# Head of a transformer step: caches loaded later, tokens turned earlier; last expert group: throw-away matmuls and one output moved up

## The reference

```python
mod = silu(c) @ w_mod + b_mod                     # c: latent or context; w_mod 1024 x 6144
shift1, scale1, gate1, shift2, scale2, gate2 = split(mod, 6)
h = rms_norm(x, g_attn) * (1.0 + scale1) + shift1
qa, ka, va, qb, kb, vb, ga, gb = split(h @ w_in)  # w_in 1024 x 4352
# attention over cached keys and values (256 tokens) and the step's own; differential
# attention with lam = exp(sum(lq1*lk1)) - exp(sum(lq2*lk2)) + 0.2
```

```python
for e in range(16):                               # expert-choice: 64 latent + 16 context rows each
    ye = silu(xe @ w_gate[e]) * (xe @ w_up[e]) @ w_down[e] * gates[e]
y[rows[e]] += gate2 * ye                          # scattered into x
out = rms_norm(y, g_final)
```

## Time and profile before

| what | value |
|---|---|
| median of three runs | 1245.5 us (1245.05 to 1246.2) |
| the profiled execution | 1246.18 us, span 1244.4 us |
| mean granted clock of TensorE | 0.981 |
| PE busy | 1188.5 us, 96% of the span |
| PE's weight loads | 854.5 us, 69% |
| DVE busy | 915.1 us, 74% |
| ACT busy | 721.6 us, 58% |
| POOL busy | 176.7 us, 14% |
| HBM read, written | 269.64 MB, 15.73 MB |

### The profile page before, as it was taken

One profiled execution on the slowest core, in us unless ns is written; L12 is line 12 of the kernel. 1 busy time (PEld: TensorE's weight loads), 2 busy tenths in 40 slices (PEclk: granted clock), 3 DMA queues, 4 the chain that ended last, 5 costly groups with the idle time before them and its releaser, 6 DMA issues.

```text
span 1244.4 us, 17367 instructions
## 1 busy us (share of the span) xinstructions
PE 1188.5 (96%) x6056; PEld 854.5 (69%) x6056; DVE 915.1 (74%) x1145; ACT 721.6 (58%) x1029; POOL 176.7 (14%) x154
## 2 busy tenths in 40 slices
PE   4899999999999999999899999999999999999994
PEld 2578877778777777778486667666676666766662
DVE  2674559899683323444778999899997999979995
ACT  3433347777641221223667876777766777667774
POOL 3143340000000000010400111100113111111110
PEclk9999999999999999999889999999999999999997
DMA  9852241110424443471648998999989999799995
GB/s 359 262 198 68 68 98 43 33 33 22 172 79 149 143 117 124 179 289 68 220 164 319 380 383 317 307 371 383 383 276 320 369 385 385 262 331 366 375 385 190
DMA packets 110862, 291.62 MB, mean 234 GB/s; under 512 B 29265, under 2 KB 30498, under 8 KB 110274
## 3 DMA queue, kind: packets, MB, share of 16 engines
q1 hardware_dynamic: 106576, 273.16, 60.5%
q0 software_dynamic: 3792, 12.86, 4.1%
q10 hardware_dynamic: 418, 4.63, 0.9%
HBM read 269.64 MB, written 15.73 MB: 229 GB/s over the span
## 4 chain that ended last, share of the span: by engine, by line
PE 88%; DVE 5%; ACT 3%; DMA 3%; issue 1%; SPq 0%; POOL 0%; ACTq 0%; DVEq 0%; POOLq 0%
PE ps L1228 14%; PE ps L1229 14%; PE ps L1230 14%; PE ps L742 9%; PE ps L744 9%; PE ps L743 9%; PE ps L956 2%; DMA raw<-in_w_mod_dram 2%; PE ps L940 2%; DVE neg_max L1861 2%; PE ps L1181 1%; PE ps L979 1%; PE ps L1182 1%; PE ps L975 1%; DVE q_lo_t L1853 1%
## 5 line engine op out<-in xcount | busy, mean ns | idle before, releaser
L1952 DVE TENSOR_TENSOR raw_lo<-raw,w_hi 128x1024 fp32r<-128x1024 f32 x256 | 304.9, 1219 | 44.6 <-ACT w_hi L1587 33.0
L1587 ACT ACTIVATE w_hi<-raw 128x1024 fp32r<-128x1024 f32 x252 | 264.8, 1059 | 80.1 <-PE ps L1230 78.4
L1228 PE MATMUL ps<-w_hi,xe_hi 128*80 128x512 f32 x512 | 204.6, 400 | 0.0
L1230 PE MATMUL ps<-w_hi,xe_lo 128*80 128x512 f32 x512 | 203.2, 397 | 0.0
L2408 POOL DMA_INDIRECT x_dram<-y_g,rows_e x15 | 87.9, 5858 | 504.4 <-DVE y_g L2181 504.4
L1952 DVE TENSOR_TENSOR extra_lo<-extra,w_hi 128x1024 fp32r<-128x1024 f32 x128 | 152.5, 1219 | 8.2 <-ACT w_hi L1587 7.3
L1587 ACT ACTIVATE w_hi<-extra 128x1024 fp32r<-128x1024 f32 x128 | 135.9, 1064 | 37.8 <-PE ps L1230 37.5
L742 PE MATMUL ps<-w_hi,ht 128*128 128x512 f32 (+1 forms) x330 | 129.5, 392 | 1.8 <-DVE ht L1754 1.8
L744 PE MATMUL ps<-w_hi,ht 128*128 128x512 f32 (+1 forms) x330 | 126.3, 383 | 0.0
L743 PE MATMUL ps<-raw_lo,ht 128*128 128x512 f32 (+1 forms) x330 | 126.2, 382 | 0.0
L522 DVE TENSOR_TENSOR raw_lo<-raw,w_hi 128x1024 fp32r<-128x1024 f32 x48 | 57.7, 1225 | 79.5 <-ACT w_hi L517 78.9
(11 more groups left out here) (322 smaller groups left out, 2026.9 us busy)
## 6 DMA issues: line engine op xcount, KB each, us to landing
raw<-in_w_exp_down_dram SPq DMA_DIRECT2D x112, 512.0 KB, 6.3
raw<-in_w_exp_gate_dram SPq DMA_DIRECT2D x80, 512.0 KB, 5.4
extra<-in_w_exp_up_dram SPq DMA_DIRECT2D x64, 512.0 KB, 5.7
raw<-in_w_exp_up_dram SPq DMA_DIRECT2D x64, 512.0 KB, 5.5
extra<-in_w_exp_gate_dram SPq DMA_DIRECT2D x48, 512.0 KB, 5.2
raw<-in_w_in_dram SPq DMA_DIRECT2D x16, 1024.0 KB, 5.5
raw<-in_w_mod_dram SPq DMA_DIRECT2D x12, 1024.0 KB, 6.8
raw<-in_w_mod_dram SPq DMA_DIRECT2D x16, 512.0 KB, 11.3
```

The lines of the kernel that those rows point to most:

```text
L1228: pe.matmul(b, stat_hi, hi[:, cols], start=(k == 0), stop=False)
L1230: mm = pe.matmul(b, stat_lo, hi[:, cols], start=False, stop=(k == KD - 1))
L1587: act.activation(w_hi[:, (DENSE_SPLITS + h) % NHL, :], expert_half(h), ACT.Copy)\
L1952: dve.tensor_tensor(expert_lo_half(h), expert_half(h), w_hi[:, (DENSE_SPLITS + h) % NHL, :].bitcast(F32), ALU.subtract).then_inc(s_lo, 1)
```

## The change

It has seven edits. (1) POOL loads the first key cache only when part chunk (1, 1) has landed, and makes the parts of the first cached keys and loads the second cache behind all its other loads. (2) ACT squares all five token tiles before it brings turned tiles out of PSUM. (3) PE's order in the head: two tokens are turned ahead of chunk (0, 1), two ahead of (0, 2), one ahead of (0, 3), `spin` matmuls whose result nobody reads stand between, the six matmuls on `w_hi` go to bank 1, part chunk (1, 0) moves ahead of `first_step(0)`. (4) The second row is turned within `first_step(2)`, between its token tiles 1 and 2. (5) The first half of the second gemm chunk is done one k tile at a time, `first_step(4)` and `first_step(5)`, so `product(0, ...)` begins with half 3. (6) DVE makes the next two low halves before the lambda sums instead of behind them. (7) In the last group PE runs 5 `spare` matmuls before the turns of expert 15's hidden rows and 6 behind them, and DVE scales expert 14's output before two splits instead of behind them.

```diff
@@ -713,7 +713,7 @@
                 nh = halves_of(j)
                 _, n, kt = GEMMS[j]
                 per = HALF // n
-                for hh in range(0 if j else 2, nh):
+                for hh in range(0 if j else 3, nh):
                     h = gemm_half(j, hh)
                     if before_half and (j, hh) != (5, 0):
                         before_half(hh)
@@ -833,21 +833,29 @@
             pe.transpose(bank(5, 0, 81), vec[:, :], ident[0:81, 0:81]).then_inc(s_vect, 1)
             pe.wait_ge(s_ct, 1)
             pe.wait_ge(s_dve, 2)
+            def spin(n):
+
+                for _ in range(n):
+                    pe.matmul(bank(1, 0, P), ident, ident, start=True, stop=True)
+
             part_chunk(0, 0)
-            part_chunk(0, 1)
-            pe.wait_ge(s_tab2, 16)
+            spin(8)
             turn_tokens(0)
             turn_tokens(1)
-            part_chunk(0, 2)
+            spin(8)
+            part_chunk(0, 1)
             turn_tokens(2)
             turn_tokens(3)
+            part_chunk(0, 2)
+            turn_tokens(4)
             part_chunk(0, 3)
-            turn_tokens(4)
+            pe.wait_ge(s_tab2, 16)
+            spin(6)
             part_turn(0)
             pe.wait_ge(s_hi, 1)
-            pe.wait_ge(s_xtd, NT)
             for _ in range(6):
-                pe.matmul(bank(5), w_hi[:, 0, 0:P], w_hi[:, 0, 0:NW], start=True, stop=True)
+                pe.matmul(bank(1), w_hi[:, 0, 0:P], w_hi[:, 0, 0:NW], start=True, stop=True)
+            part_chunk(1, 0)
 
             def hth(k, tt):
                 return ht[:, HT_HI[k], tt]
@@ -873,28 +881,32 @@
                     turn_keys(("b", 1, 0))
                     turn_keys(("b", 1, 1))
 
-            def first_step(k):
+            def first_step(k, between=None):
 
                 h = gemm_half(0, k // 2)
                 pe.wait_ge(s_lo, SPLIT_OF[h] + 1)
                 pe.wait_ge(s_htl, k + 1)
                 hi, lo = hi_half(h, NW)[:, k % 2, :], lo_half(h, NW)[:, k % 2, :]
                 for t in range(NT):
+                    if t == 2 and between:
+                        between()
                     b, tt = bank(t), slice(t * P, (t + 1) * P)
                     pe.matmul(b, hth(k, tt), hi, start=(k == 0), stop=False)
                     pe.matmul(b, hth(k, tt), lo, start=False, stop=False)
                     mm = pe.matmul(b, htl(k, tt), hi, start=False, stop=False)
                 return mm
 
+            pe.wait_ge(s_xta, NT)
+            pe.wait_ge(s_xtd, NT)
             first_step(0)
-            part_chunk(1, 0)
             part_chunk(1, 1)
             first_step(1)
             part_chunk(1, 2)
             part_chunk(1, 3)
-            first_step(2)
-            part_turn(1)
+            first_step(2, between=lambda: part_turn(1))
             first_step(3).then_inc(s_half, 4 // 2)
+            first_step(4)
+            first_step(5).then_inc(s_half, 1)
             product(0, hth, htl, before_half=lambda hh: pe.wait_ge(s_htl, 2 * hh + 2))
             turn_keys(("a", 0, 0))
             turn_keys(("b", 0, 0))
@@ -1219,6 +1231,12 @@
                                           ident[0:EROWS, 0:EROWS])
                     mm.then_inc(s_htr, 1)
 
+                def spare(n):
+
+                    for _ in range(n):
+                        pe.matmul(bank(0, 0, EG * EROWS, slice(0, EROWS)), xe_hi[:, 0, 0:EROWS], xe_hi[:, 0, :],
+                                  start=True, stop=True)
+
                 def half_product(h, banks, stat_hi, stat_lo, k, sides=(0, 1)):
                     pe.wait_ge(s_lo, i * GH + DENSE_SPLITS + h + 1)
                     hi, lo = w_hi[:, (DENSE_SPLITS + h) % NHL, :], expert_lo_half(h)
@@ -1249,8 +1267,13 @@
                                 pe.wait_ge(s_silu2, i * 8 + 2 * EG)
                                 gather_context(i + 1)
                                 gather(i + 1, 0)
+                            if last:
+                                pe.wait_ge(s_silu2, i * 8 + 2 * EG)
+                                spare(5)
                             turn_hidden(e, 0)
                             turn_hidden(e, 1)
+                            if last:
+                                spare(6)
                             if not last:
                                 gather(i + 1, 1)
                                 gather(i + 1, 2)
@@ -1301,10 +1324,8 @@
                 if t:
                     act.wait_ge(s_ss, t)
                 act.activation(squares[:, :], x_n[:, t, :], ACT.Square, accum_out=ss[:, t:t + 1]).then_inc(s_ss, 1)
-                if t >= 2:
-                    evict_tokens(t - 2)
-            evict_tokens(NT - 2)
-            evict_tokens(NT - 1)
+            for t in range(NT):
+                evict_tokens(t)
             split_hi(act, SPLITS[0])
             act.wait_ge(s_xta, NT)
             act.wait_ge(s_xtd, NT)
@@ -1780,6 +1801,7 @@
                                          ALU.mult)
 
 
+            lead(0, HALVES_B, 2)
             dve.wait_ge(s_bc, 16 * 6)
             dve.tensor_scalar(g_qk[:, 0, :], g_qk[:, 0, :], SCALE, None, ALU.mult).then_inc(s_dve, 1)
             own()
@@ -1788,8 +1810,6 @@
             dve.wait_ge(s_dve, own())
             dve.tensor_reduce(lam[:, 0:2 * HB].rearrange("p (a h) -> p a h", a=2), pairs[:, :, 0], AX.X, ALU.add)\
                .then_inc(s_lamw, 1)
-
-            lead(0, HALVES_B, 2)
             dve.wait_ge(s_lame, 1)
             dve.tensor_tensor(lam[:, 2 * HB:], lam[:, 0:HB], lam[:, HB:2 * HB], ALU.subtract).then_inc(s_dve, 1)
             dve.wait_ge(s_dve, own())
@@ -2192,9 +2212,12 @@
                         if before == "u" and k == 0:
                             hidden(e1, 0)
                             hidden(e1, 1)
+                        early = last and (before, e1) == ("d", EG - 2)
+                        if early and k == 0:
+                            output(e1)
                         if not last or h + LEAD < GH:
                             expert_lo(h + LEAD, i)
-                        if before == "d" and k == 1 and (n or not first):
+                        if before == "d" and k == 1 and (n or not first) and not early:
                             output(e1)
                         if before == "u" and kind == "g" and k in (4, 5):
                             hidden_lo(e1, k - 4)
@@ -2271,7 +2294,6 @@
                 pool.dma_start(k_cache[:, KVA:, :].rearrange("p m d -> p (m d)"),
                                cache_diff_k[0, 0, rows].rearrange("p h i d -> p (h i d)")).then_inc(s_kc[n], 16)
 
-            load_key_cache(0)
             def one_over_rms(dst, sums, count_of, semaphore):
 
                 pool.tensor_scalar(dst, sums, 1.0 / count_of, EPS, ALU.mult, ALU.add).then_inc(s_pool, 1)
@@ -2305,10 +2327,9 @@
                     make_parts(("b", n, g), k_cache[:, KVA + 4 * g:KVA + 4 * g + 4, :])
 
 
-            pool.wait_ge(s_kc[0], 32)
-            make_cached_parts(0)
-            pool.wait_ge(s_kparts, 3)
-            load_key_cache(1)
+            second_half = CHUNK["part", 1, 1]
+            pool.wait_ge(s_raw[second_half % NRAW], raw_count[second_half])
+            load_key_cache(0)
             for n, src in enumerate((lambda_q1, lambda_k1, lambda_q2, lambda_k2)):
                 flat = src.rearrange("a h d -> a (h d)")
                 pool.dma_start(lam_w[:, n, :, :].rearrange("p h d -> p (h d)"), flat.to_broadcast([P, HB * HD]))\
@@ -2319,6 +2340,10 @@
                 .then_inc(s_vac, 16)
             pool.dma_start(vb_n[:, 0:2, :], cache_diff_v[0, 0].rearrange("(t p) h d -> p t (h d)", p=P))\
                 .then_inc(s_vc, 16)
+            pool.wait_ge(s_kc[0], 32)
+            make_cached_parts(0)
+            pool.wait_ge(s_kparts, 3)
+            load_key_cache(1)
 
             for t in range(NT):
                 pool.wait_ge(s_qss, t + 1)

```

## The result

The changed kernel took 1238.49 us (median of five, 1237.35 to 1240.56), the kernel before 1245.25 us beside it (1243.32 to 1246.2): ratio 0.9946, 95% interval 0.9932 to 0.996. Forecast: 1239.0.

A forecast was written before the change was run, and what follows sets the result against it. The prediction took the head to be bound by DMA, with PE carrying 88% of the chain. Head -5.0 and last group -1.6 sum to -6.6: 1245.5 - 6.6 = 1238.9, say 1239 us; range 1233.5 to 1242.5.

The forecast's parts named there:

- bound by DMA at (1, 3): Head, second row's last chunk: lands at 37.4 instead of 45.05 us, read from 37.8; 6.3 us won.
- part_turn(0) at 24.5: Head, first row's turn on PE: runs at 24.5 us instead of 29.71, with spins filling idle time.
- The hole: Slow DMA stretch while g_qk loads finish: moves to 39.0 to 43.0 us, so chunk (gemm 0, 1) lands at 46.5.
- Idle 4.1 us, clock cost 1.8: Ahead of first_step(4): PE stands from 46.7 to 50.8 us, then slow matmuls cost 1.8 (0 to 2.5).
- The cap: ACT's squares behind the lambda sums: square 4 at 65.9 us, product 1 no earlier than 67.3, 6.0 below 73.25.
- Head -5.0, tail -1.6: Product 0 ends at 66.6 instead of 71.65 us; last group's spare matmuls hold the clock, saving 1.6.
- A: Head: slow stretch does not follow g_qk loads, (gemm 0,1) lands at 42.7, head -9.7, time 1234 us; chance 0.22.
- B: Head: (1,3) stays behind the hole, landing at 45; time 1240.7 us; chance 0.12.
- C: Head, slower: the hole grows, meeting three waiting chunks; 1248 us with a hole of 13 us; chance 0.04.
- D: Nothing measurable: lower clock also behind find_rows at 802, last group's drop may stay; 1243.9 us; chance 0.07.

The follow-up runs named there:

- the list alone: Kernel before with only GpSimd's (POOL's) new load order, first key cache after part chunk (1, 1): 1243.28 us, ratio 0.9985.
- three traces: Traces of three versions of the changed kernel: no spare matmuls (1238.32 us), lambda sums first (1237.59), expert 14's output late (1237.53).
- The version with all rows different: Changed kernel with all six lambda and g_qk loads reading 128 different rows instead of one row 128 times; computes other values; ran once, 1237.98 us.
- the version with the loads moved away: Changed kernel with all six one-row loads (four lambda, two g_qk) moved behind the second key cache: 1232.97 us, ratio 0.9913.
- the version with GpSimd's old list: Changed kernel with GpSimd's (POOL's) load order put back as in the kernel before, the other edits kept: 1243.09 us, ratio 0.9987.
- one version: Changed kernel with only the two g_qk loads reading 128 different rows instead of one row 128 times; computes other values; ran once, 1234.94 us.

## Why the prediction was right, point by point

**The kernel is bound by DMA at (1, 3), and the list frees it.** Right as to the landing: forecast 37.4, measured 37.2. But it reads as if the 6.3 us were won by the list, and the list alone won 1.9. PE waited only 0.71 us for this chunk before, and what makes its early landing pay is PE's new order.

**part_turn(0) at 24.5.** Wrong by 1.8: it ran at 26.26, though chunk (0, 0) began 0.7 us earlier than before (9.63 for 10.32) where the working has it "as before". I counted a spin as one instruction of 0.12 us; it is two, and the second group took 1.95 us for what I put at 1.0. By the trace without spins, they push part_turn(0) by 2.2 us and pay 0.6 back at part_turn(1).

**The hole moves onto (gemm 0, 1), which lands at 46.5.** The mechanism was right, and the landing at 46.2 to 46.4 in three traces. In the profiled one it was 45.0. I tied the hole to the g_qk loads alone, but the lambda loads make half of it. The Trainium skill (DMA: Bandwidth & Descriptors, Why small descriptors are slow) puts the bus overhead of a 256-byte descriptor at 27%, so small rows cost little by it. The version with all rows different agrees, at 320 GB/s and more; that rule is about size and does not speak of one row read again and again, which is what made the hole here.

**Idle 4.1 us, clock cost 1.8.** The end of the wait was forecast at 50.8 and came at 50.5 to 50.7 in the three traces. PE got there later, so it waited 2.2 to 2.3, not 4.1, and the low clock still came and cost 1.54. In the profiled execution of the changed kernel the wait was 0.42 and there was no low clock. This is the step that missed in that trace: 1.5 us of the end of the wait (49.28 for 50.8) and 1.8 of the clock, 3.2 in all at the first key turn (63.40 for 66.6), of which 0.6 went into the longer wait for ACT.

**The cap.** Forecast: square 4 can't come earlier than 19.4 us behind the landing (65.9 less 46.5). Measured: 64.23 - 45.0 = 19.2. It bound, at 1.03 us of wait, in the trace where PE was fast. So the b turn is 7.6 earlier there.

**Head -5.0, tail -1.6.** In the three traces the b turn is 5.3 to 5.5 us earlier, and the tail 1.53 in the changed kernel: -6.9, beside 6.8 between the medians. In the profiled execution -7.6 and -1.5, so there the forecast was some 2.5 short. That the other executions of the changed kernel are like the three traces is likely and not shown, and low-clock stretches outside the head, which the forecast took as fixed, move traces against each other by up to 3 us. That the number came within 0.5 us is in part luck.

**Rivals.** A named 1234 for a hole not tied to g_qk. It was tied to them and to the lambda loads, so A did not come. That the version with the loads moved away reached 1232.97 is another mechanism, and in its trace only 2.1 us of it lie in the head. B did not come: (1, 3) got ahead of the hole. C did not come here, but the version with GpSimd's old list shows its mechanism, a hole on a chunk without cover. D did not come: at 944 and 1094 us the low clock stayed as before, but the last group's drop was gone. What D feared does happen: the stretch that the kernel before lacks at 802 is there at 795.0 in the trace with the lambda sums first and at 798.1 in the one with the late output, which in turn has none near 944.

## What to carry to other kernels

Look for a load that reads one row of HBM to all partitions, and put it where no needed chunk is in flight: here even two of 32 KB held up the chunks in the other queue. A transfer that is moved takes its stall along, so ask which chunk it will lie on next, and how many us of cover that chunk has. Where executions differ by more than an edit is worth, compare the same stretch in several traces, not the medians alone; and follow a gain along the trace to see how much of it arises where the edit is.

## What the runs showed of the hardware

- 64 KB and 512 KB read as one row 128 times cut the queues to 59 to 283 GB/s for some 5 us in the changed kernel (33 at the lowest in the kernel before); from different rows the rate stayed at 320 GB/s or more.
- With PE at full clock before the wait, the clock fell to 1.2 GHz after waits of 2.2 to 2.3 us ahead of first_step(4), and stayed after 1.08 and 0.42 us there. It fell, too, about the last group's eight short turns with pauses of 0.82 and 1.04 us around them. Length alone does not decide: 1.94 us at 34.20 in the kernel before kept the clock, 1.20 us at 27.24 in one version lost it, and the same 1.33 us past 590 us lost it in five traces of fourteen.
- The low stretch behind first_step(4) cost 1.54 us.
- The landing of the same chunk moved by 1.4 us (45.0 to 46.4) between traces with the same loads in the head.
- A plain fp32 matmul of 128x128 is two instructions in the trace: 16 for eight calls, 1.95 us at the full clock.
